# GpSimd makes the first block's low weights, and the first blocks and loads are re-ordered

## What is computed

```python
mod = silu(c) @ w_mod[l] + b_mod[l]                      # sh1, sc1, g1, sh2, sc2, g2
h = rmsnorm(x, norm1_g[l]) * (1 + sc1) + sh1
q, k, v, ca, cb, su, gates = split(h @ w_in[l])
y_attn = sliding_window_attention(rope(q), rope(k), v) @ w_attn_o[l]
y_conv = conformer_conv(ca, cb, ...)                     # GLU, 31 taps, layernorm, silu, projection
y_ssm  = s5_ssm(su, a, dt, B, C, d, ...)                 # diagonal complex scan, GLU
x = x + g1 * ((gate_a * y_attn + gate_c * y_conv + gate_s * y_ssm) @ w_out[l])
h2 = rmsnorm(x, norm2_g[l]) * (1 + sc2) + sh2
x = x + g2 * ((silu(f_gate) * f_up) @ w_ffn_out[l])
```

## Time and profile before

| | |
|---|---|
| median of 3 runs | 933.24 us (932.68 to 933.51) |
| the profiled execution's own time | 935.88 us |
| its span | 934.1 us |
| mean granted TensorE clock in it | 0.996 of full speed |
| instructions | 15663 |

### The profile page before, as it was taken

The page is one execution under the profiler, slowest core; times in us unless marked ns, Lnnn a source line. Parts: engine busy times, 40 slices in busy tenths (PEclk is TensorE's granted clock), DMA queues, the critical chain, the costliest instruction groups (busy, mean ns, idle before and its releaser), DMA issues.

```text
span 934.1 us, 15663 instructions
## 1 busy us (share of the span) xinstructions
PE 905.1 (97%) x6575; PEld 763.9 (82%) x6575; DVE 708.7 (76%) x941; ACT 486.4 (52%) x606; POOL 12.8 (1%) x13
## 2 busy tenths in 40 slices
PE   5999999999999999999999999999999999999996
PEld 1898977777778999899988998777777888888885
DVE  3896898998677688676677689998957766666666
ACT  4794248743737674655345316883373643343334
POOL 2000000000000000000000000000000000000001
PEclk9999999999999999999999999999999999999999
DMA  8993366657896559847977534445778455555531
GB/s 355 241 275 122 134 223 226 232 203 280 303 262 222 176 177 334 315 141 241 311 258 166 156 133 136 140 149 196 257 296 293 157 194 190 181 180 192 195 109 46
DMA packets 128566, 196.10 MB, mean 210 GB/s; under 512 B 30730, under 2 KB 90642, under 8 KB 122352
## 3 DMA queue, kind: packets, MB, share of 16 engines
q1 hardware_dynamic: 126119, 194.89, 62.2%
q10 hardware_dynamic: 2376, 0.21, 0.2%
HBM read 194.02 MB, written 1.06 MB: 209 GB/s over the span
## 4 chain that ended last, share of the span: by engine, by line
PE 81%; DVE 8%; SPq 3%; DMA 3%; ACT 3%; issue 2%; ACTq 0%; DVEq 0%
PE bank L617 19%; PE bank L619 18%; PE bank L618 18%; PE bank L983 8%; PE bank L984 4%; PE bank L655 3%; DVE wlo L1570 2%; PE bank L721 2%; DVE yc L1880 1%; SPq L591 1%; DMA raw<-in_w_in 1%; DMA raw<-in_w_mod 1%; PE bank L745 1%; PE bank L733 1%; PE bank L903 1%
## 5 line engine op out<-in xcount | busy, mean ns | idle before, releaser
L1570 DVE TENSOR_TENSOR wlo<-raw,whi 128x2048 fp32r<-128x2048 f32 (+1 forms) x136 | 302.6, 2227 | 145.3 <-PE bank L619 73.2
L1176 ACT ACTIVATE whi<-raw 128x2048 fp32r<-128x2048 f32 x133 | 251.3, 1896 | 102.0 <-DMA raw<-in_w_in 51.4
L617 PE MATMUL bank<-hb,whi 128*128 128x256 f32 x592 | 170.4, 288 | 1.1 <-DVE wlo L1570 1.1
L619 PE MATMUL bank<-hb,wlo 128*128 128x256 f32 x592 | 167.6, 283 | 0.0
L618 PE MATMUL bank<-hb,whi 128*128 128x256 f32 x592 | 167.5, 283 | 0.0
L617 PE MATMUL bank<-whi,bhi 128*128 128x512 f32 x304 | 121.2, 399 | 0.3 <-DVE blo L1987 0.3
L983 PE MATMUL bank<-hb,whi 128*128 128x512 f32 x336 | 119.0, 399 | 0.0
L619 PE MATMUL bank<-whi,blo 128*128 128x512 f32 x304 | 118.8, 391 | 0.0
L618 PE MATMUL bank<-wlo,bhi 128*128 128x512 f32 x304 | 118.6, 390 | 0.0
L617 PEld LDWEIGHTS bank<-hb,whi 128*128 128x128 f32 x592 | 113.4, 192 | 3.9 <-DVE wlo L1570 1.7
L618 PEld LDWEIGHTS bank<-hb,whi 128*128 128x128 f32 x592 | 113.5, 192 | 0.4
(11 more groups left out here) (277 smaller groups left out, 1126.3 us busy)
## 6 DMA issues: line engine op xcount, KB each, us to landing
raw<-in_w_mod SPq DMA_DIRECT2D x48, 1024.0 KB, 5.5
raw<-in_w_ffn_in SPq DMA_DIRECT2D x44, 1024.0 KB, 5.1
raw<-in_w_in SPq DMA_DIRECT2D x38, 1024.0 KB, 7.2
raw<-in_w_ffn_out SPq DMA_DIRECT2D x22, 1024.0 KB, 5.0
raw<-in_w_out SPq DMA_DIRECT2D x8, 1024.0 KB, 7.5
raw<-in_w_in SPq DMA_DIRECT2D x16, 256.0 KB, 4.6
raw<-in_ssm_glu_b SPq DMA_DIRECT2D x4, 1024.0 KB, 6.3
raw<-in_ssm_glu_a SPq DMA_DIRECT2D x4, 1024.0 KB, 5.2
```

The costliest lines, as they stand in the source:

```text
L617: mm(o, w_hi, a_hi, start=start, stop=False, skip_group_check=True)
L619: return mm(o, w_lo, a_hi, start=False, stop=stop, skip_group_check=True)
L1176: fn(whi[mi % N_HI][:, n], raw[SLOT[item]][:, n], ACT.Copy).then_inc(hi_half if half == 0 else s_hi, 1)
L1570: part = V.tensor_tensor(wlo[mi % N_LO][:, n], raw[SLOT[("main", *divmod(mi, NB))]][:, n], whi[mi % N_HI][:, n].bitcast(F32), ALU.subtract)
```

## The change

- The loads of c, identity and constants move from SP to ACT, ahead of ACT's small vectors, so SP's first issue is the first mod item.
- Block 0's weights are loaded in two halves with a semaphore for the first. ACT makes the high half in two pieces: piece 0, two pieces of `norm_hi`, piece 1, six pieces of `norm_hi`.
- GpSimd makes block 0's low weights, DVE no longer does. PE runs block 0 as high x `hhi`, high x `hlo`, low x `hhi`.
- Block 1 runs as high x (`hhi`, `hlo`), then the two C rounds, then low x `hhi`. ACT's doubling of C and the eight C copies move into block 1, ahead of `hi(3)`.
- C and b_re are loaded behind block 2's weights (before: ahead of them), with the late constants and the taps.
- `b_source(0, 0)` moves to block 0 and `b_source(0, 1)` to block 1 on DVE; `b_spread(0, 0)` moves from block 0 to block 1 on ACT.
- The last filler goes from 17 to 7 matmuls.
- In both layers `softmax_scale` of round 3 moves ahead of `hi` of block 18.

```diff
-B_SPREAD_AT = [{0: 0, 2: 1}, {PREP_AT + 6: 1}]
+B_SPREAD_AT = [{1: 0, 2: 1}, {PREP_AT + 6: 1}]
...
-def lo_engine(i):
-    return "dve"
+def lo_engine(l, i):
+    return "pool" if (l, i) == (0, 0) else "dve"
...
         def _(sp):
-            sp.dma_start(crow[:, :], A["c"].rearrange("b (r c) -> (b r) c", c=P)).then_inc(s_c, 16)
-            sp.dma_start(ident[:, :], A["c_ident"]).then_inc(s_const, 16)
-            sp.dma_start(consts[:, :], A["c_small"]).then_inc(s_const, 16)
...
-                if item == ("main", 0, 2):
+                if item == ("main", 0, 3):
                     load_c(sp, 0)
                     load_b(sp, 0, 0)
-                if item == ("main", 0, 3):
                     late_constants(sp)
                     load_taps(sp, 0)
...
+                    if item == ("main", 0, 0):
+                        ((d, src),) = main(0, 0, dst)
+                        sp.dma_start(d[:, 0:4], src[:, 0:4]).then_inc(s_first, 16)
+                        sp.dma_start(d[:, 4:8], src[:, 4:8]).then_inc(landed, 16)
...
+                        if mi == 0 and k == 4:
+                            pe.wait_ge(s_hi, 1)
                         pe.wait_ge(hhi_ready, h0 + k + 1)
...
-                    if mi == 0:
-                        pe.wait_ge(s_lo[lo_engine(0)], LO_NO[(0, 0)] + 1)
-                        for k in range(DK):
-                            for c in range(2):
-                                mm(o[:, c * T:(c + 1) * T], w8[1][:, k, c * P:(c + 1) * P], hhi[:, k, :], start=False, stop=False, skip_group_check=True)
-                        for r in range(2):
-                            prep_round(0, r)
                     for k in range(DK):
                         pe.wait_ge(hlo_ready, h0 + k + 1)
...
+                    if mi == 0:
+                        pe.wait_ge(s_lo[lo_engine(0, 0)], LO_NO[(0, 0)] + 1)
+                        for k in range(DK):
+                            for c in range(2):
+                                last = mm(o[:, c * T:(c + 1) * T], w8[1][:, k, c * P:(c + 1) * P], hhi[:, k, :], start=False, stop=(k == DK - 1),
+                                          skip_group_check=True)
+                    last.then_inc(s_unit, 1)
+                elif mi == 1:
+                    o = unit_bank(l, i)
+                    for k in range(DK):
+                        for c in range(2):
+                            for a in (hhi, hlo):
+                                mm(o[:, c * T:(c + 1) * T], w8[0][:, k, c * P:(c + 1) * P], a[:, k, :], start=(k == 0 and c == 0 and a is hhi), stop=False,
+                                   skip_group_check=True)
+                    for r in range(2):
+                        prep_round(0, r)
+                    middle()
+                    pe.wait_ge(s_lo[lo_engine(l, i)], LO_NO[(l, i)] + 1)
...
-            keep_busy(bank[0], 17)
+            keep_busy(bank[0], 7)
...
                 if l == 0:
+                    pool.wait_ge(s_hi, 1)
+                    nc.gpsimd.tensor_tensor(wlo[0][:, :], raw[SLOT[("main", 0, 0)]][:, :], whi[0][:, :].bitcast(F32),
+                                            ALU.subtract).then_inc(s_lo["pool"], 1)
                     continue
...
-                if t - 2 in SCORES_AT:
+                if t - 2 in SCORES_AT and SCORES_AT[t - 2] < 3:
                     softmax_scale(l, SCORES_AT[t - 2])
...
-            hi(0)
-            norm_hi(0, 0, DK)
+            hi(0, 0)
+            norm_hi(0, 0, 2)
+            hi(0, 1)
+            norm_hi(0, 2, DK)
             hi(1)
-            act.wait_ge(s_cc[0], 32)
-            fn(once[:, :, 1, :], once[:, :, 0, :], ACT.Copy).then_inc(c_twice, 1)
-            for n in range(2):
-                round_copy(0, n)
             for l in range(DEPTH):
                 for i in range(NB):
                     side(l, 2 * i)
...
+                    if (l, i) == (0, 1):
+                        act.wait_ge(s_cc[0], 32)
+                        fn(once[:, :, 1, :], once[:, :, 0, :], ACT.Copy).then_inc(c_twice, 1)
+                        for n in range(2):
+                            round_copy(0, n)
...
+                    if SCORES_AT.get(2 * i - 1) == 3:
+                        softmax_scale(l, 3)
                     if i < NB - 1:
                         hi(l * NB + i + AHEAD)
...
-                if n == 0:
-                    lo(0)
...
-            b_source(0, 0)
...
-                    if (l, i) == (0, 0):
-                        b_source(0, 1)
+                    if l == 0 and i < 2:
+                        b_source(0, i)
```

More of the change, by code:

```diff
@@ L255 @@
 for _e in ("pool", "dve"):
-    for _n, _m in enumerate([(l, i) for l in range(DEPTH) for i in range(NB) if lo_engine(i) == _e]):
+    for _n, _m in enumerate([(l, i) for l in range(DEPTH) for i in range(NB) if lo_engine(l, i) == _e]):
         LO_NO[_m] = _n
@@ L562, in _ @@
                 if was and was[0] == "main":
-                    e = lo_engine(was[2])
+                    e = lo_engine(was[1], was[2])
                     sp.wait_ge(s_lo[e], LO_NO[(was[1], was[2])] + 1)
@@ L589, in _ @@
                         load_taps(sp, 1)
-                    for d, src in main(item[1], item[2], dst):
-                        sp.dma_start(d, src).then_inc(landed, 16)
+                    if item == ("main", 0, 0):
+                        ((d, src),) = main(0, 0, dst)
+                        sp.dma_start(d[:, 0:4], src[:, 0:4]).then_inc(s_first, 16)
+                        sp.dma_start(d[:, 4:8], src[:, 4:8]).then_inc(landed, 16)
+                    else:
+                        for d, src in main(item[1], item[2], dst):
+                            sp.dma_start(d, src).then_inc(landed, 16)
                     if item[1] == 0 and DEPTH > 1 and item[2] == AT[("fg", 0)]:
@@ L914, in main_block @@
                         for c in range(2):
-                            last = mm(o[:, c * T:(c + 1) * T], w8[0][:, k, c * P:(c + 1) * P], hlo[:, k, :], start=False, stop=(k == DK - 1),
+                            last = mm(o[:, c * T:(c + 1) * T], w8[0][:, k, c * P:(c + 1) * P], hlo[:, k, :], start=False, stop=(mi > 0 and k == DK - 1),
+                                      skip_group_check=True)
[12 more added lines that the diff above has]
+                                mm(o[:, c * T:(c + 1) * T], w8[0][:, k, c * P:(c + 1) * P], a[:, k, :], start=(k == 0 and c == 0 and a is hhi), stop=False,
+                                   skip_group_check=True)
+                    for r in range(2):
+                        prep_round(0, r)
+                    middle()
+                    pe.wait_ge(s_lo[lo_engine(l, i)], LO_NO[(l, i)] + 1)
+                    for k in range(DK):
+                        for c in range(2):
+                            last = mm(o[:, c * T:(c + 1) * T], w8[1][:, k, c * P:(c + 1) * P], hhi[:, k, :], start=False, stop=(k == DK - 1),
                                       skip_group_check=True)
@@ L1136, in _ @@
                 nc.gpsimd.tensor_copy(once[:, :, 1, :], once[:, :, 0, :]).then_inc(c_twice, 1)
-            for l in range(DEPTH):
-                for i in range(NB):
-                    if lo_engine(i) != "pool":
-                        continue
-                    mi = l * NB + i
-                    pool.wait_ge(s_hi, mi + 1)
-                    if mi >= N_LO:
-                        pool.wait_ge(s_unit, used(mi - N_LO))
-                    nc.gpsimd.tensor_tensor(wlo[mi % N_LO][:, :], raw[SLOT[("main", l, i)]][:, :], whi[mi % N_HI][:, :].bitcast(F32),
-                                            ALU.subtract).then_inc(s_lo["pool"], 1)
             pool.wait_ge(s_final_g, 16)
@@ L1171, in hi @@
                 item = ("main", *divmod(mi, NB))
-                act.wait_ge(s_land[SLOT[item]], LANDED[item])
+                if mi == 0 and half == 0:
+                    act.wait_ge(s_first, 16)
+                else:
+                    act.wait_ge(s_land[SLOT[item]], LANDED[item])
                 if mi >= N_HI:
@@ L1465, in side @@
                     taps_copy(l + 1)
+            act.dma_start(crow[:, :], A["c"].rearrange("b (r c) -> (b r) c", c=P)).then_inc(s_c, 16)
+            act.dma_start(ident[:, :], A["c_ident"]).then_inc(s_const, 16)
+            act.dma_start(consts[:, :], A["c_small"]).then_inc(s_const, 16)
             small_vectors(act, 0)
```

12 lines of the change are left out of this document (7 added, 5 removed).

## The result

The changed kernel takes 938.13 us (median of 4 runs, 936.48 to 938.43), the kernel before 933.38 beside it (932.68 to 933.68). The ratio is 1.0041, 95% interval 1.0029 to 1.0053: slower by 2.7 to 4.9 us, 3.8 in the middle. The two medians lie 4.75 us apart, near the upper end of that. The forecast was 933.7, the range ended at 936.6, and slower by over 0.2% had a chance of 0.30. The profiled execution after took 938.21 us, its span is 936.4.

What follows compares the result with a forecast made beforehand. PE bounds the kernel, busy 905.1 of 934.1 us, so only its work or waits count. +2.1 + 1.9 - 1.75 - 1.8 = +0.45 us, carried onto the timed median 933.2, gives 933.7; range 930.3 to 936.6.

Steps and rivals of the forecast that it cites:

- part 4: Layer 1, softmax_scale of round 3 ahead of hi(18): PE's wait goes, -1.75 us, and the low clock, -1.8 us.
- part 1: Start: three small loads leave SP, first w_mod issue at 0.72 instead of 2.06, -1.34 us; norm at 29.2, before 30.56.
- With the wait goes the low clock behind it: -1.8: Layer 1, behind PE's wait for the scaled probabilities: the low clock goes too, -1.8 us, bounds 0 and -2.
- no refund: Rival, chance 0.24: layer 1's low clock may belong to the profiled execution alone; gain only 1.75 us, sum +2.25, 935.5.
- delay only the first of them, with later transfers queued behind it: Start: ACT's three more issues, 0.4 us each, delay only the first of the DMA-paced modulation blocks.
- Part 2: Block 0 re-ordered: GpSimd subtracts in 4.6 us, holding DVE's low norm until 36.1; block 1 ends 48.1, before 48.3.
- ACT free at 48.6: Block 1: ACT's eight small C copies, 2.65 us, follow the C transposes and leave ACT free at 48.6.
- my bound of 3.7: Upper bound on the +1.9 us clock loss of block 2, if block 0's own 2 us gap costs it too.
- The 45.5 given for a DVE that is not held: End of block 1 if GpSimd's subtraction does not hold DVE's low norm steps: 45.5 instead of 48.1.
- Part 3: C and B behind block 2's weights, spread behind hi(3): B transposes +2.1 us, low clock after block 2's 4 us gap +1.9.
- X: Moment block 3's weights have landed: 50.9 before, forecast 50; bounds 46.7 early, 48.3 to 51.4 late; break-even 47.9.
- Their users have 3 us and more: DVE's b_source(0, 1), rope angles and c_powers come 1.5 us later against PE; their users have 3 us or more.

Runs made afterwards that it cites:

- experiment 10: Changed kernel with C and B loaded early, b_spread(0, 0) and C's doubling, rounds and copies back in block 0: 933.22 us, 0.9997 against before.
- experiment 4: Changed kernel with C and B loaded ahead of block 2's weights, b_source(0, 0) ahead of block 0, b_spread(0, 0) in block 0: 936.29 us, 1.0026.
- experiment 7: Changed kernel with b_spread(0, 0) ahead of hi(3), DVE making block 0's low weights, b_source(0, 1) ahead of lo(3): 933.66 us, 0.9995 against before.
- experiment 12: Changed kernel with softmax_scale of round 3 put back behind hi(18): 941.79 us, 1.0082 against before.
- Experiment 1: Kernel before with only softmax_scale of round 3 moved ahead of hi(18): 932.14 us, 0.9978 against before.
- Experiments 2: Changed kernel with the loads of c, identity and constants back on SP, 7 fillers kept: 938.22 us, 1.0048 against before.
- experiment 9: Kernel before with softmax_scale of round 3 ahead of hi(18) and the three small loads on ACT's queue, 17 fillers kept: 931.90 us, 0.9977.
- experiment 3: Changed kernel with DVE instead of GpSimd making block 0's low weights, behind its low norm steps: 939.03 us, 1.0054 against before.
- experiment 5: Changed kernel with b_spread(0, 0) ahead of hi(3) in ACT's program, loads in their new order: 939.14 us, 1.0049 against before.
- experiment 8: Changed kernel with unused filler matmuls in PE's two gaps, in block 0 and in block 2: 936.19 us, 1.0030 against before.
- 11: Kernel before with softmax_scale of round 3 ahead of hi(18) and b's load moved behind block 2's weights, C staying ahead: 933.18 us, 0.9987.

## Why the prediction was wrong

Four kernels form a chain from the good to the bad, each one group of edits on. Ratios against before: part 4 alone 0.9978; with part 1 and GpSimd (experiment 10) 0.9997; with the C rounds in block 1 (experiment 4) 1.0026; with C and B behind block 2's weights (the changed kernel) 1.0041. The steps are 1.8, 2.7 and 1.4 us, 5.9 together, each uncertain by about 1.3, so that the last may be nothing; and part 4 takes off 2.05. They are prices in this order: experiment 7 takes another way from the changed kernel and wins back as much. Parts 1 to 3 without part 4 (experiment 12, 1.0082) cost 7.7 us, which agrees with 5.9 only within the noise.

- *"With the wait goes the low clock behind it: -1.8"* is the step that failed most. Experiment 1 gives 2.05 us for part 4 where the forecast had 3.55, since the low clock stood in one execution of four. The rival "no refund" (0.24) named it, with 935.5. I had noticed that the profiled execution was 2.6 us longer than the timed ones, and still summed against it as if its clock were everybody's.
- *Part 1, -1.34 us* has the wrong sign. The issue moved, but "delay only the first of them, with later transfers queued behind it" assumed that the three loads land later only by the time of their issue, about 1 us. The last landed 5.6 us later than before, and the first block's delay went on to all that follow, since SP waits for its buffer. The norm came 0.7 us later and not 1.34 earlier. Experiments 2 and 9 show no cost of this in the time; but against the forecast all of part 2 started 2.1 us late by it.
- *Part 2*: size and mechanism of GpSimd's work were right (4.56 us for 4.6; DVE held until it ended). The low norm steps took 6.93 us beside GpSimd and 3.25 without it (experiment 3). The rule of the Trainium skill, "SBUF — State Buffer", section "Who interferes with whom", that a DVE instruction with two SBUF inputs contends with a GpSimd instruction that reads SBUF, agrees with that. What was wrong is "ACT free at 48.6". It was 51.1, since block 0 ended at 44.2 and not 41.4: 2.1 us of this are the late start, the rest is the low clock over its passes, my bound of 3.7, which I had left out of the sum. (The 45.5 given for a DVE that is not held is 44.9 by the same steps; nothing hangs on it.)
- *Part 3*: X was 50.8 for 50 (block 2's weights came 3.3 us earlier and not 6). The chain behind it stood as worked out, except that the C copies, and not X, ended last ahead of `hi(3)`. "Their users have 3 us and more", on `b_source(0, 1)`, was wrong: it was hidden only behind the first wait, as experiment 5 shows. The place of t = 7 was forecast 2.1 + 1.9 = 4.0 us later and came 4.7 later. Of that, 1.3 us is the clock in block 2 (8.87 us from t = 5 to t = 7, less the 7.55 of experiment 8), for the 1.9 of the sum: PE's wait there was 2.5 us and not 4, since block 1 ended at 50.6 and not 48.1.
- *Part 4* did what it says: no wait of PE at that line.
- Not in the forecast at all: PE's stalls with no releaser add up to 2.05 us after and 0.96 before. The one near 528 (0.28 to 0.83 us) stands ahead of the last 24 of 128 small matmuls in the changed kernel and in experiments 2 to 7, 10 and 12, which all have 6555 matmuls; the kernels with the 6575 of before (1, 9, 11) don't have it, nor has experiment 8, with 6603. In three profiled executions the clock fell near that place, in experiments 7 and 12 behind this stall, in 8 without it. No run was made on why PE stands there, but the traces point to one thing. The DMA view has 52 loads of instructions of 16 KB on queue q8, and each of the 28 stalls with no releaser in the fourteen profiles ends 2.4 to 2.8 us after one of them starts (89.6 and 525.4 in the changed kernel, for stalls that end at 92.12 and 527.95; 83.6 before, for 86.13). So PE seems to wait for the next piece of its own program, where it runs through many short instructions, and 20 matmuls fewer move the places at which the pieces end. That is argued and not tested.

The sum with what was measured: +4.7 at t = 7, -2.05, +1.1 of stalls is +3.75; the ratio says +3.8, the medians +4.75. Against the forecast's +0.45 that is 1.5 us for the refund that did not come, 0.7 at t = 7 and 1.1 for the stalls. That it meets the ratio to 0.1 us is luck, since one profile gives t = 7 only to within about 1 us (experiment 12).

No kernel tried beats part 4 alone (932.14 us, 0.22% under the kernel before); that with part 1 on top (931.90) can't be told from it.

## What to carry to other kernels

A job moved "into the shade" must be checked on the engine that does it, not only on the one that waits: the C copies had stood in ACT's idle time before block 2's weights and were moved to just ahead of `hi(3)`, where other work waits for ACT. When a wait is taken away, list what stands behind it on every engine's program; the second wait (`b_source` behind `lo(3)`) was longer than the first. And before a clock loss of one profiled execution goes into a sum, compare that execution's clock and time with those of the other runs.

## What the hardware showed

- The granted clock fell to half behind waits of PE of 1.7, 2.5, 2.9 and 4.1 us in the start and of 1.87 in layer 1, each time for 3 to 7 us. It did not fall behind waits of 1.5 us (experiments 4 and 10), nor behind two of 1.84, one in block 3 (experiment 9) and one in layer 1 (experiment 12). In three executions it fell at 518 to 529 where PE had last stood for only 0.56, 0.69 and 0.83 us (experiments 7, 8 and 12). So for a wait near 1.8 us a profile of one execution doesn't tell what the next will do. Fillers held the clock at 1.00 in both gaps of the start.
- The granted clock in the windows doesn't tell all: before 16 us it reads 1.00 in the kernel before, yet the eight matmuls of a mod item at 12.47 took 1.93 us, and those at 24.91 took 1.06.
- Of three small loads that had landed by 3.6 us from SP's queue, the last landed at 9.2 from ACT's, though they were issued within 2.2 us of the start. Beside them ran the bulk that SP now issued first; whether the other queue or the bulk ahead of them is the reason was not separated.
- GpSimd subtracts 128x2048 in 4.56 us, DVE in 2.29, and a DVE step with two SBUF inputs that is issued meanwhile ends only after it: eight steps of 0.4 us took 6.93.
